# Hybrid decoder step on one Trainium2 core: the two heads of a pair as one burst of matmuls on both halves of the array

## The reference, cut to what matters

```python
for g, (win, dil) in enumerate(B_PATTERNS):          # (128,1), (512,4), (2048,16)
    o, lse = banded_window_attn(qb[:, :, g, :, None, :], kb[:, :, g], vb[:, :, g], dil)
    outs.append(o); lses.append(lse)
o_b = combine_dilations(outs, lses)                  # softmax over lses, weighted sum of outs
hp_next = finish_layer(hp, o_a, o_b, ga, gb, *rest)  # gates, branches, w_out, norm, MLP, norm
```

## Time and profile before

| what | value |
|---|---|
| median of 3 runs | 1868.54 us (1868.33 to 1870.34) |
| the profiled execution's own time | 1867.71 us |
| its span | 1866.1 us |
| TensorE busy in the span | 98% |
| mean granted TensorE clock | 0.995 of full |
| the stage with full unit traffic | about 395 to 690 us |

### The profile page before, as it was taken

One profiled execution on the slowest core, in us unless ns is written; L12 is line 12 of the kernel. 1 busy time (PEld: TensorE's weight loads), 2 busy tenths in 40 slices (PEclk: granted clock), 3 DMA queues, 4 the chain that ended last, 5 costly groups with the idle time before them and its releaser, 6 DMA issues.

```text
span 1866.1 us, 33466 instructions
## 1 busy us (share of the span) xinstructions
PE 1824.5 (98%) x12746; PEld 1769.6 (95%) x12746; DVE 968.1 (52%) x1320; ACT 785.5 (42%) x1098; POOL 112.7 (6%) x216
## 2 busy tenths in 40 slices
PE   7999999999999999999999999999999999999995
PEld 7999999997888889999899999999999999999995
DVE  5545443365555554655766544555345543455564
ACT  5445543454555554333534422333323333244332
POOL 0000000111111111100000000000000000000002
PEclk9999999999999999999999999999999999999998
DMA  8455555685666655655455566566666666666741
GB/s 261 144 153 153 165 168 163 183 304 193 251 204 219 237 207 190 214 176 166 151 203 203 186 237 210 202 205 221 223 206 214 202 215 205 216 213 200 247 138 67
DMA packets 270994, 369.34 MB, mean 198 GB/s; under 512 B 11984, under 2 KB 264592, under 8 KB 267968
## 3 DMA queue, kind: packets, MB, share of 16 engines
q1 hardware_dynamic: 252544, 251.79, 43.7%
q0 software_dynamic: 9088, 106.90, 14.9%
q10 hardware_dynamic: 9280, 9.51, 1.5%
HBM read 356.02 MB, written 70.71 MB: 229 GB/s over the span
## 4 chain that ended last, share of the span: by engine, by line
PE 94%; DVE 2%; ACT 1%; POOL 1%; issue 1%; DMA 0%; POOLq 0%; SPq 0%; ACTq 0%; DVEq 0%
PE psM L1166 29%; PE psM L1167 29%; PE psM L1168 29%; PE psM L1214 1%; PE psO L1261 1%; PE psT L1240 1%; PE psM L1227 1%; PE psO L1274 1%; DVE s_wlo L773 1%; POOL s_r L445 0%; PE psT L1186 0%; PE psO L1276 0%; PE psO L1271 0%; PE psM L1218 0%; PE psO L1289 0%
## 5 line engine op out<-in xcount | busy, mean ns | idle before, releaser
L773 DVE TENSOR_TENSOR s_wlo<-s_raw,s_whi 128x1024 fp32r<-128x1024 f32 x468 | 569.4, 1225 | 617.0 <-ACT s_whi L459 612.5
L459 ACT ACTIVATE s_whi<-s_raw 128x1024 fp32r<-128x1024 f32 x468 | 490.7, 1057 | 781.9 <-PE psM L1168 761.1
L1166 PE MATMUL psM<-s_xhi,s_whi 128*128 128x320 f32 x1248 | 391.9, 314 | 10.3 <-DVE s_xlo L778 9.6
L1167 PE MATMUL psM<-s_xlo,s_whi 128*128 128x320 f32 x1248 | 386.7, 310 | 0.0
L1168 PE MATMUL psM<-s_xhi,s_wlo 128*128 128x320 f32 x1248 | 386.6, 310 | 0.0
L1166 PE MATMUL psM<-s_ghi,s_whi 128*128 128x322 f32 x1024 | 319.1, 312 | 6.6 <-DVE s_wlo L773 6.6
L1167 PE MATMUL psM<-s_glo,s_whi 128*128 128x322 f32 x1024 | 319.9, 312 | 0.0
L1168 PE MATMUL psM<-s_ghi,s_wlo 128*128 128x322 f32 x1024 | 319.1, 312 | 0.0
L1166 PE MATMUL psM<-s_uhi,s_whi 128*128 128x320 f32 x1024 | 316.9, 309 | 0.0
L1168 PE MATMUL psM<-s_uhi,s_wlo 128*128 128x320 f32 x1024 | 316.4, 309 | 0.0
L1167 PE MATMUL psM<-s_ulo,s_whi 128*128 128x320 f32 x1024 | 316.4, 309 | 0.0
(11 more groups left out here) (196 smaller groups left out, 1670.7 us busy)
## 6 DMA issues: line engine op xcount, KB each, us to landing
s_raw<-in_w_ff_dram SPq DMA_DIRECT2D x256, 512.0 KB, 4.0
s_raw<-in_w_in_dram SPq DMA_DIRECT2D x156, 512.0 KB, 3.9
s_kvbuf<-in_kT_b_dram POOLq DMA_DIRECT2D x8, 2448.0 KB, 9.0
s_kvbuf<-in_v_b_dram POOLq DMA_DIRECT2D x8, 2304.0 KB, 8.3
s_raw<-in_w_out_dram SPq DMA_DIRECT2D x32, 512.0 KB, 3.4
out_b_s_dram<-in_cache_b_kv_dram POOLq DMA_DIRECT2D x16, 1008.0 KB, 6.4
s_raw<-in_w_branch_a_dram SPq DMA_DIRECT2D x16, 512.0 KB, 3.4
gates_scratch<-s_gstage ACTq DMA_DIRECT2D x16, 320.0 KB, 3.6
```

Of the source, the lines that this page charges most:

```text
L459: act.activation(whi[:, slot], raw[:, slot], ACT.Copy).then_inc(hi_done, 1)
L773: dve.tensor_tensor(wlo[:, slot], raw[:, slot], whi[:, slot].bitcast(F32), ALU.subtract).then_inc(lo_done, 1)
L1166: pe.matmul(out, wh, hi[:, t0 + k], start=first and k == 0, stop=False)
L1167: pe.matmul(out, wh, lo[:, t0 + k], start=False, stop=False)
```

## The change

The order of the units changes: the two heads of a pair follow one another within a query block, (B,0,0), (B,1,0) at the start of a cycle and (B,0,1), (B,1,1) in its middle. A, SB and SA keep their places.

The values of both heads are computed in the second head's turn, alternating head by head, each into its own 64 partitions of one bank; the first head's turn has no values. The probabilities of both lie in the two halves of `PT`. One copy of 128 partitions then takes both out of PSUM, and `outs(U)` gives the number of copies made by the units before U, for the waits on `o_out`.

For the first query block the scores of both heads are computed in the first head's turn, alternating, one on array rows 0 to 63 and one on 64 to 127, each into its own bank of `psM[0]`; the second head's turn has no scores. For the second query block each head's scores are computed in its own turn, as before.

```diff
-        UNITS = [("B", 0, 0), ("B", 0, 1), ("A", 0, 0), ("A", 0, 1), ("SB", 0, 0), ("SA", 0, 0),
-                 ("B", 1, 0), ("B", 1, 1), ("A", 1, 0), ("A", 1, 1), ("SB", 1, 0), ("SA", 1, 0)]
+        UNITS = [("B", 0, 0), ("B", 1, 0), ("A", 0, 0), ("A", 0, 1), ("SB", 0, 0), ("SA", 0, 0),
+                 ("B", 0, 1), ("B", 1, 1), ("A", 1, 0), ("A", 1, 1), ("SB", 1, 0), ("SA", 1, 0)]
...
+        def waits_for_partner(k):
+
+            return UNITS[k][0:2] == ("B", 0)
+
+        def outs(U):
+
+            return sum(not waits_for_partner(V % NU) for V in range(U))
...
-            pool.wait_ge(o_out, 4 * NU)
+            pool.wait_ge(o_out, outs(LAST))
...
             def o_evac(j, k, U):
 
                 kind, e, qb = UNITS[k]
+                if waits_for_partner(k):
+                    return
...
-                    part = slice(64 * e, 64 * e + 64) if kind == "B" else slice(0, P)
                     tile = j + (8 if kind == "B" else 4 * e)
-                    last = act.activation(oT[part, tile, P * qb:P * qb + P], ps[part, 0:P], ACT.Copy)
+                    last = act.activation(oT[:, tile, P * qb:P * qb + P], ps[:, 0:P], ACT.Copy)
...
-                act.wait_ge(o_out, LAST)
+                act.wait_ge(o_out, outs(LAST))
...
-                    last = dve.scalar_tensor_tensor(Sp[:, 0:n].rearrange("p (g k) -> p g k", g=3), ps[:, 0:3, 0:nk], SCALE, pm,
-                                                    ALU.mult, ALU.add)
+                    got = psM[0][:, e, 0:n].rearrange("p (g k) -> p g k", g=3) if qb == 0 else ps[:, 0:3, 0:nk]
+                    last = dve.scalar_tensor_tensor(Sp[:, 0:n].rearrange("p (g k) -> p g k", g=3), got, SCALE, pm, ALU.mult, ALU.add)
...
+                if (kind, e, qb) == ("B", 1, 0):
+                    return
...
-                if kind == "B":
+                if kind == "B" and qb == 0:
+
+                    for g in range(3):
+                        for h in range(2):
+                            half = slice(64 * h, 64 * h + 64)
+                            mm = pe.matmul(psM[0][:, h, P * g:P * g + P], qTb[half, 4 * g + j, qs], kTb[half, 4 * g + j, 0:P], start=True, stop=True)
+                            if g == 2:
+                                mm.then_inc(scores, 1)
+                    return
+                elif kind == "B":
...
             def unit_values(j, k, U):
                 kind, e, qb = UNITS[k]
+                if waits_for_partner(k):
+                    return
...
-                wait(pe, o_out, U - 1)
+                wait(pe, o_out, outs(U - 1))
                 if kind == "B":
+
                     for t in range(nb):
                         g, kb = divmod(t, qb + 1)
-                        mm = pe.matmul(out[64 * e:64 * e + 64, 0:P], vnat[:, kb, P + 512 * g + P * j + 64 * e:P + 512 * g + P * j + 64 * e + 64], PTk[:, t * P:t * P + P],
-                                       start=t == 0, stop=t == nb - 1)
+                        for h in range(2):
+                            col = P + 512 * g + P * j + 64 * h
+                            mm = pe.matmul(out[64 * h:64 * h + 64, 0:P], vnat[:, kb, col:col + 64], PT[:, (k + 1 + h) % 2, t * P:t * P + P],
+                                           start=t == 0, stop=t == nb - 1)
+                            if t == nb - 1:
+                                mm.then_inc(pv, 1)
+                    return
```

## The result

The change makes the kernel faster: 1857.03 us median (1856.52 to 1858.17, 4 runs) against 1869.44 us (1868.33 to 1870.42, 4 runs), ratio 0.9935 with a 95% interval of 0.9917 to 0.9952.

A forecast was written before the change was run, and what follows sets the result against it. TensorE's queue was taken as the bound (98% busy). Savings of 4 x (0.85 + 2.23) = 12.3 us, plus 0.2 for entry, less 0.2 for keys, gave 1868.5 - 12.3 = 1856.2 us, range 1854 to 1861.

The forecast's parts named there:

- The bursts: TensorE's B units: shared bursts save 0.85 us (first-block scores) and 2.23 us (values) a cycle, over four cycles.
- Entering and leaving: TensorE's bursts: a chunk directly followed by sample values saves between 0 and 0.6 us more; taken at 0.2.
- The sample keys: GpSimd's key load before TensorE's sample scores: slack falls from 1.17 to 0.05 us; stall 0 to 3 us, taken at 0.2.
- The rivals with late keys: Tight key loads 1 to 2 us longer, 1858 to 1862 us (chance 0.07); all seven later loads stalling, slower (0.03).
- The wait at the start: TensorE's 0.7 us wait for a gate's sigmoid at the stage's start: between 0 and 0.7 us gained, taken as 0.
- Nothing else became late: TensorE's stage: no wait added; probabilities ending at 498.5 us stay early for transposes at 510.2, since a step saves below 2 us.
- the rule of the Trainium skill cited in the prediction: Weight loads overlap matmuls in flight only when the row group differs; values would gain nothing, time some 1865 us.

The follow-up runs named there:

- e1: The change, but each head's first-block scores in its own turn again (shared values bursts kept): 1860.44 us, ratio 0.9953 to before.
- e2: The change, but each head's values and their copy in its own turn again (shared score bursts kept): 1865.14 us, ratio 0.9978 to before.
- e3: The change with only the new order of units, scores and values in their own turns: 1869.40 us, ratio 1.0001 to before.
- e4: The change, but both heads' values go to output partitions 0 to 63, head after head, with two copies out: 1864.05 us, ratio 0.9976 to before.
- e5: The change, but both heads' first-block scores use array rows 0 to 63: 1857.77 us, ratio 0.9946 to before.
- e6: The change without alternation, all matmuls of the first head, then the second's, each on its own half: 1862.91 us, ratio 0.9970 to before.
- e9: The change, but residual passes in the MLP's first block over 2 tiles after each of eight groups, not 4 after four: 1850.50 us, ratio 0.9900.
- e10: The change with both the late copies of e7 and the half residuals of e9: 1848.24 us, ratio 0.9887 to before.
- e7: The change, but GpSimd's twelve copies of new keys and values to the outputs issued after the attention: 1857.14 us, ratio 0.9936 to before.
- e8: The kernel before the change, with the same late copies as e7: 1869.21 us, ratio 1.0003 to before.

## Why the prediction was right

**The bursts.** Scores 0.86 + 0.86 to 0.87 and values 4.50 to 0.81 + 1.46 us a cycle, both as forecast to 0.01 us. e1 to e3 show that these two terms carry the gain (2.24 and 1.04 us a cycle), and e4 to e6 that it is the halves, taken in turn.

**Entering and leaving.** Taken at 0.2 us over four cycles, bounded at 0.6. Undisturbed cycles fell by 3.29 us where the bursts explain 3.08: 0.2 us a cycle, 0.8 in all, beyond the bound. It shows in the first matmul of the sample values (1.05 to 0.86 us), and it comes with the scores: e2's cycle fell by 1.04, their burst by 0.85. The bound was mis-sized, as it took the 0.15 us of a values burst for the crossings around a scores burst.

**The sample keys.** In the third load the last copy again ended 14.15 us after the issue; GpSimd's first issue, first copy and last copy, and TensorE's sample scores:

```profile
460.19 0.54 POOL L359 DMA_DIRECT2D s_kvbuf<-in_kT_b_dram  x1 [17.30 <-PE psO L1304]
...
472.51 1.22 POOL L378 COPY s_kca<-s_kTa 128x8 f32<-128x8 f32 x1 [11.24 <-DMA s_kca<-in_kT_a_dram]
...
473.82 0.52 POOL L382 COPY s_kvbuf<-s_kTb 128x128 f32<-128x128 f32 x2
```

```profile
474.49 0.35 PE L1243 MATMUL psM<-s_kvbuf,s_QbS 128*128 128x136 f32 x1
```

473.82 + 0.52 = 474.34 us, and the scores at 474.49: 0.15 us between them, with the burst at 1.09 instead of 0.93 us. Before the slack was 1.17, and 0.05 was forecast. The second cycle's loss of 0.16 us against the others (76.40 to 76.24) is this; the other loads kept 2.15 us or more. The rivals with late keys did not come. But the prediction took the 14.15 us for the load's own time, and they are not: the transfers had landed 12.27 us after the issue. GpSimd's first copy then lasted 1.22 us, where it lasts 0.19 behind the change's other loads, and it ended 0.05 us after a subtraction of VectorE (L782, 472.46 to 473.68 us). Before, the first copy lasted 0.77 us and ended in the same way behind L773, which is how the same 14.15 can come again. So 1.0 of the 14.15 us is not the transfers', and by this sum TensorE would not have waited without it. In e9 and e10 the first copy lasted 0.19 us, the keys were complete 11.57 and 11.96 us after the issue, and no cycle lost the 0.16.

**The wait at the start.** "Between 0 and 0.7 us is gained" was the step that failed. The 0.7 us went, but I had looked only at the table load and the exponentials ahead of the sigmoid, and not at what stood in ScalarE's queue behind it: a weight chunk for which ScalarE already waited 1.81 us before the change, unnoticed by TensorE. The chunk came no later than before (ScalarE took it up at 392.67 us, before at 392.86), but TensorE was earlier, and it waited 1.7 us. e7 and e8 show its cause; in e7 the first cycle takes 69.54 us, 4.10 less than before, so without the wait 0.8 us would have been gained beyond the 3.29.

**How much of the agreement is luck.** The two misses, 0.6 us more from the crossings and 1 us less in the first cycle, nearly cancel. The attention fell by 12.04 us and the profiled span by 11.1; that the medians fell by 12.4, within 0.1 of the forecast, is chance, since the MLP part alone moves by 1.5 us and more between executions.

**Nothing else became late.** No other wait of TensorE appeared in the stage, as the slacks said.

By the rule of the Trainium skill cited in the prediction (TensorE: Matmul & The Clock Gate, Part 3, on weight loads and row groups), taken alone, the values could have gained nothing; the halved busy time of L1286 disagrees, and sides with the speedups for column tiles that the same section lists and the prediction left out. The same section calls matmuls strictly first in, first out. e6 disagrees, its second head beginning ahead of the last three records of the first; but only so far.

## What to carry to other kernels

If small matmuls use half of the array's rows or output columns, look for a second set that uses the other half, and issue the two alternately: here two bursts then cost what one had cost (0.81 us for twelve records against 0.80 for six), priced by the chain's pieces and not by the sum of latencies. Not every interleaving does it; here blocks of up to 4 records overlapped fully and longer ones began late, so a burst of the same kernel that overlaps "anyway" may be just short enough.

When a stage gets shorter, check each queue for what it already waits for at a fixed time, such as the weight chunk here: a wait that cost nothing before is the first to show. A wait of one engine can also end by another's work, as GpSimd's key copy did by VectorE's subtraction, so look at what ended it before calling it a transfer's time.

## What was not expected of the hardware

TensorE ran matmuls of the other half out of their order in the queue, within some 4 records (e6: from the ninth record of 12 on; 2.38 us against 1.46 alternated).

A small copy of GpSimd (the first after a key load) lasted 0.47 to 1.24 us instead of 0.19 in ten loads of eight traces, before and after the change among them, and ended each time 0.05 us behind a VectorE subtraction that was under way.

The clock fell to its lower level behind one of several waits of 1.8 to 2.6 us, not always the same one (e2's first cycle; the MLP part before and after the change), and cost about 1.5 us where TensorE had work. With the four residual waits gone (e9) the 105 us behind the two that remain ran at the full clock. A wait of TensorE of 1.8 us thus cost 3.3 where the clock fell behind it, and this is a source of scatter between executions.
